# A recurrent branch pipelined one step ahead: the next input product in thirds between this step's gate products

## The reference, cut to what matters

```
z = xn @ w_in;  u_x, u_g, ... = split(z)
conv_in  = concatenate([conv_hist, u_x])              # 3 frames of history
u        = conv1d(conv_in, conv_w, width 4, per channel) + conv_b
r        = sigmoid(blockdiag(u, w_a) + b_a)           # 64 x 64 blocks
i        = sigmoid(blockdiag(u, w_x) + b_x)
log_a    = -8 * r * softplus(-lru_lambda);  a = exp(log_a)
b        = sqrt(-expm1(2 * log_a)) * (i * u)
h[t]     = a[t] * h[t-1] + b[t]                       # a scan along time
y        = gelu(u_g) * h                              # then @ w_rnn_out, elsewhere
```

## Time and profile before

| | us |
|---|---|
| median of 3 runs | 2535.72 |
| profiled execution, its own time | 2537.56 |
| its span, first to last instruction | 2535.7 |
| attention stages before the recurrent stage, up to about | 1268 |
| recurrent stage, first matmul 1269.27 to the next stage's first DMA 1535.98 | 266.7 |
| TensorE clock granted, mean over the span | 0.936 |

### The profile page before, as it was taken

How to read it: one execution, slowest core, us unless ns; L and a number is a source line. 1 busy time by engine, 2 the same in 40 slices (tenths; PEclk the granted TensorE clock), 3 DMA queues, 4 the chain that set the end, 5 groups by cost and what they waited for, 6 DMA issues and landing times. The chain is left out here.

```text
span 2535.7 us, 36826 instructions
## 1 busy us (share of the span) xinstructions
PE 2175.3 (86%) x11116; PEld 1764.4 (70%) x11116; DVE 1345.9 (53%) x1576; ACT 1130.0 (45%) x1539; POOL 227.3 (9%) x299
## 2 busy tenths in 40 slices
PE   4469898988889797699999998998938999999993
PEld 2357676766767674499988888997836777777772
DVE  5423635455463545421145563224266888888885
ACT  3223444435343443221146663113215777777771
POOL 0210202012020201000000000000000010100003
PEclk9779999999999997799999998999968999999996
DMA  3310302021120201121132323131138999999996
GB/s 92 68 36 10 86 9 77 25 61 42 44 76 9 69 25 36 57 89 42 33 89 89 91 85 122 41 131 67 42 118 288 393 394 395 392 398 392 398 392 243
DMA packets 199024, 351.66 MB, mean 139 GB/s; under 512 B 19700, under 2 KB 127400, under 8 KB 198872
## 3 DMA queue, kind: packets, MB, share of 16 engines
q1 hardware_dynamic: 181496, 293.55, 32.4%
q0 software_dynamic: 13872, 44.74, 5.8%
q10 hardware_dynamic: 3584, 12.58, 1.2%
HBM read 301.87 MB, written 48.97 MB: 138 GB/s over the span
## 5 line engine op out<-in xcount | busy, mean ns | idle before, releaser
L2466 DVE TENSOR_TENSOR e_w_lo<-e_raw,e_w_hi 128x2048 fp32r<-128x2048 f32 x189 | 427.6, 2290 | 83.2 <-ACT e_w_hi L2396 43.5
L2396 ACT CAST e_w_hi<-e_raw 128x2048 fp32r<-128x2048 f32 x189 | 360.9, 1911 | 50.6 <-PE e_y_ps L103 33.6
L101 PE MATMUL proj_ps<-w_qkv_hi,xh 128*128 128x384 f32 x544 | 233.1, 429 | 24.8 <-PEq L287 19.1
L101 PE MATMUL ux_ps<-xh,r_wx_hi 128*128 128x364 f32 x576 | 192.2, 334 | 25.6 <-DVE r_wx_lo L777 14.8
L102 PE MATMUL ux_ps<-xl,r_wx_hi 128*128 128x364 f32 x576 | 191.2, 332 | 0.0
L103 PE MATMUL ux_ps<-xh,r_wx_lo 128*128 128x364 f32 x576 | 191.1, 332 | 0.0
L103 PE MATMUL proj_ps<-w_qkv_hi,xl 128*128 128x384 f32 x544 | 188.4, 346 | 0.0
L102 PE MATMUL proj_ps<-w_qkv_lo,xh 128*128 128x384 f32 x544 | 188.2, 346 | 0.0
L1353 PE MATMUL out_ps<-mT 128*128 128x512 f32 (+3 forms) x384 | 170.9, 528 | 2.9 <-DVEq L84 2.3
L101 PEld LDWEIGHTS proj_ps<-w_qkv_hi,xh 128*128 128x128 f32 x544 | 106.9, 197 | 51.4 <-issue 45.2
L1552 ACT ACTIVATE mT<-st_ps 128x512 f32<-128x512 f32 x192 | 93.9, 489 | 103.8 <-PE st_ps L1338 48.8
(11 more groups left out here) (431 smaller groups left out, 5087.1 us busy)
## 6 DMA issues: line engine op xcount, KB each, us to landing
e_raw<-w_gate_e SPq DMA_DIRECT2D x64, 1024.0 KB, 7.3
e_raw<-w_up_e SPq DMA_DIRECT2D x64, 1024.0 KB, 7.9
e_raw<-w_down_e SPq DMA_DIRECT2D x64, 1024.0 KB, 7.4
w_raw<-w_in SPq DMA_DIRECT2D x24, 512.0 KB, 4.6
r_wx<-w_in SPq DMA_DIRECT2D x24, 512.0 KB, 3.9
slot_y<-e_y ACTq DMA_DIRECT2D x32, 384.0 KB, 6.1
slot_y<-zrows POOLq DMA_DIRECT2D x24, 368.0 KB, 4.4
mT<-cache_k SPq DMA_DIRECT2D x8, 1024.0 KB, 5.7
```

What stands on the lines that cost most here:

```text
L101: nc.tensor.matmul(out, a_hi, b_hi, start=start, stop=False)
L2396: sc.copy(w_hi[u][:, :], w.raw[c][:, :]).then_inc(wh_ready, 1)
L2466: v.tensor_tensor(w_lo[u][:, :], w.raw[c][:, :], w_hi[u][:, :], ALU.subtract).then_inc(wl_ready, 1)
```

## The change

PE runs the input product one step ahead and cuts it into three thirds. Behind each third it issues two of this step's six gate units. So its loop is now: gelu product of step c (`branch`), then third 0 of the input product of step c+1, gate units 0 and 1 of step c, third 1, units 2 and 3, third 2 (signals `ux_ready`), units 4 and 5. The input product of step 0 stands ahead of the loop; step 7 has only its gelu product and its six units.

ACT waits for the gelu product first, rounds the next g weights, loads the sigmoid table, does sigmoids 0 and 1, then gelu (moved from behind tanh), the sigmoid table again, sigmoids 2 and 3, the copies of the next step's `ux_ps` (`take_input`, for step c+1), sigmoids 4 and 5, exp, tanh, the rounding of the x weights of step c+2, and the square root. The wait for `step_done` moves from unit 0 to gelu and unit 3.

DVE does `rest_g` for c+1, i times u, then the convolution of step c+1 (`convolve`), then the two operations for the root, `rest_x` for step c+2, then i times the root, the scans and y. The chains are split: `chain_i` for the copies, `chain_u` for the convolution. SP and POOL keep their lists. The arithmetic of every operation is the same. The core of the diff (bodies that are only moved into functions are left out):

```diff
-        V_STEPS, A_STEPS = 19, 15
+        chain_u, chain_i = sem("r_chain_u"), sem("r_chain_i")
+        V_STEPS, U_STEPS, A_STEPS = 9, 10, 10
...
             @block.tensor
             def _(pe):
...
+                def gate_unit(c, m):
+                    if m == 0:
+                        pe.wait_ge(bd_loaded, c * 64 + 64)
+                        pe.wait_ge(u_ready, c + 1)
+                    c0, n = CHUNKS[m % 3]
+                    pe.wait_ge(gate_taken, c * GATE_UNITS + max(m - 1, 0) + 1)
+                    nc.tensor.matmul(gate_ps[:, m % 2, 0:n], bd[:, m // 3, :], u_sb[:, c0:c0 + n],
+                                     start=True, stop=True).then_inc(gate_ready, 1)
+
+                def branch(c):
+                    pe.wait_ge(g_split, c + 1)
+                    pe.wait_ge(gel_ready, c + 1)
                     for j in range(N_THIRDS):
+                        last = third_of(ug_ps, wg_split, j)
+                    last.then_inc(ug_ready, 1)
+
+                def next_input(c):
+                    pe.wait_ge(x_split, c + 2)
+                    pe.wait_ge(conv_ready, c + 2)
+                    for j in range(N_THIRDS):
+                        last = third_of(ux_ps, wx_split, j)
+                        if j == N_THIRDS - 1:
+                            last.then_inc(ux_ready, 1)
+                        for m in range(j * 2, j * 2 + 2):
+                            gate_unit(c, m)
...
+                with pe.Fori(0, KT - 1) as c:
+                    branch(c)
+                    next_input(c)
+                branch(KT - 1)
+                for m in range(GATE_UNITS):
+                    gate_unit(KT - 1, m)
...
+                def step(c, more, after):
+                    chain = Chain(act, chain_a, c * A_STEPS)
+                    vec = lambda v: g.chan[:, bass.ds(c + v * KT, 1)]
+                    act.wait_ge(ug_ready, c + 1)
                     if more:
+                        round_g(c + 1)
                     chain(nc.scalar.activation(warm[:, :], g.ident[:, 0:1], ACT.Sigmoid))
...
+                    unit(0)
+                    unit(1)
+                    if more:
+                        gelu()
+                    chain(nc.scalar.activation(warm[:, :], g.ident[:, 0:1], ACT.Sigmoid))
+                    unit(2)
+                    unit(3)
+                    if more:
+                        take_input(c + 1)
+                    unit(4)
+                    unit(5)
                     act.sem_inc(ri_ready, 1)
...
+                    if not more:
+                        gelu()
+                    if after is not None:
+                        after()
                     act.wait_ge(var_ready, c + 1)
                     chain(nc.scalar.activation(v_sb[:, :], v_sb[:, :], ACT.Sqrt, scale=-1.0), std_ready)
...
+                take_input(0)
+                round_x(1)
+                with act.Fori(0, KT - 2) as c:
+                    step(c, True, lambda: round_x(c + 2))
+                step(KT - 2, True, round_gate)
+                step(KT - 1, False, None)
...
+                def step(c, more, after):
+                    chain = Chain(dve, chain_v, c * V_STEPS)
+                    vec = lambda k: g.chan[:, bass.ds(c + k * KT, 1)]
                     if more:
+                        rest_g(c + 1)
                     dve.wait_ge(ri_ready, c + 1)
                     chain(v.tensor_tensor(i_sb[:, :], i_sb[:, :], u_sb[:, :], ALU.mult))
+                    if more:
+                        convolve(c + 1)
 
                     dve.wait_ge(at_ready, c * 2 + 2)
                     chain(v.tensor_tensor(v_sb[:, :], a_sb[:, :], a_sb[:, :], ALU.mult))
                     chain(v.scalar_tensor_tensor(v_sb[:, :], v_sb[:, :], 1.0, th_sb[:, :], ALU.add, ALU.mult), var_ready)
+                    if after is not None:
+                        after()
                     dve.wait_ge(std_ready, c + 1)
...
                 rest_g(0)
+                convolve(0)
+                rest_x(1)
+                with dve.Fori(0, KT - 2) as c:
+                    step(c, True, lambda: rest_x(c + 2))
+                step(KT - 2, True, rest_gate)
+                step(KT - 1, False, None)
```

## The result

| | before | after |
|---|---|---|
| median of 4 runs each, us | 2536.73 | 2559.36 |
| lowest to highest | 2534.19 to 2538.62 | 2558.36 to 2560.05 |
| span of the profiled execution | 2535.7 | 2556.7 |
| stage: first matmul to the next stage's first DMA | 266.7 (1269.27 to 1535.98) | 289.5 (1268.92 to 1558.43) |
| one step, us | 30.8 | 31.9 (the first), then 33.6 to 34.4 |

The ratio is 1.0092, 95% interval 1.0079 to 1.0105: slower by 0.9%. The medians differ by 22.6 us, and the stage alone became 22.8 us longer, which is all of it.

What follows compares the result with a forecast made beforehand. PE bounded the kernel before (busy 29.2 of 31.0 us per step); after, a 32.2 us loop through PE, ACT and DVE would. 2537.56 + 13.4 for the later stage end + 9.2 for the clock gave 2560 us, range 2547 to 2568.

Steps and rivals of the forecast that it cites:

- the rest of the path: Stage up to the end of y(7), without a clock change: 13.4 us later than before, giving 2551.0 us.
- part 6: PE's clock falls after each idle before third 0: 1.5 us in each of six loops, 9.2 us in all.
- Part 1: PE's order: waits for `gate_taken` vanish; third 0 to third 2 takes 15.4 us, a step 28.7 if PE never waits.
- Part 2: Loop between `next_input` calls through PE, ACT's copies and sigmoids, and DVE to `rest_x`: 32.2 us against 30.8.
- The idle: PE waits for `x_split` in front of each `next_input` but the first, about 3.4 us.
- Part 3: Nothing else is later: x load hidden by 5 us; gelu's wait for y costs nothing, 0.9 us in hand.
- Part 4: ACT's extra table load per step lies in idle time before the copies; costs nothing, without that cover 2.4 us.
- Part 5: Stage ends: y(6) at 1524.9 releases step 7's i sigmoids; y(7) ends at 1541.8, 13.4 us later than before.
- the fourth rival: Clock stays low 4.9 us or more per idle before third 0: 2564 us, 2568 with gate units stretched; chance 0.06.
- the one in which the clock stays up: Same loop, but the clock stays up or falls in few loops: 2551 us; chance 0.30.
- PE sets the pace: At the `x_split` wait before third 0: ACT and DVE's list fits under 13.4 us, loop 28.7, 2530 us; chance 0.06.

Runs made afterwards that it cites:

- the remainder moved: The changed kernel with DVE making the remainder of the x weights straight behind the convolution, ahead of the root's two operations; 2535.19 us, ratio 0.9994.
- early x weights: The changed kernel with x weights of step c+2 loaded before the gate-unit wait, rounded behind sigmoid 5, remainder made behind i times u; 2533.61 us, ratio 0.9993.
- early g weights: The kernel with early x weights, and ACT rounds the g weights of step c+2 ahead of the square root of step c; 2531.23 us, ratio 0.9977.
- the last two kernels: Early x and g weights plus an own tile for the last step's i sigmoids, 2531.91 us; early x and g plus one-column gelu behind sigmoid 1, 2522.42 us.
- The tile of its own: The kernel with early x and g weights, with the last step's i sigmoids going to a separate tile; 2531.91 us, ratio 0.9980.
- the last kernel: The kernel with early x and g weights plus a one-column gelu behind sigmoid 1 that loads gelu's table before y; 2522.42 us, ratio 0.9946.

## Why the prediction was right

2560 us were forecast and 2559.36 came; the mechanism is the one of the forecast in each part that a run could reach. That the number came within 1 us is luck: the price of the clock, put at 9.2 us, was 13.3, and the rest of the path, put at 13.4, was 9.1 (part 6).

- **Part 1, PE's own work.** Forecast 28.7 us a step, measured 31.93 - 3.99 = 27.94. The gate units were taken too long: units 4 and 5 with the switch take 0.99 us (1341.93 to 1342.92), where the sum had 1.5 at the most careful reading of the earlier trace rows. From the earlier trace rows a pair of 512 was put at 1.8 us and a 64 at 0.6; a 64 with a 512 unit takes about 1 us rather than 1.4.
- **Part 2, the loop.** Forecast 32.2 us, measured 31.93 in the one loop at full clock. PE's part with its handover was 14.98 us (15.4 + 0.14 forecast), ACT's 4.06 us (3.86 + 0.14 forecast) and DVE's with the handover to PE 12.89 (12.56 + 0.14). That `rest_x` at its new place sets it is shown by moving it: the loss is gone.
- **The idle** was 4.0 us for 3.4: PE's own work was 0.8 us shorter than forecast, the loop only 0.3 us.
- **Part 3.** ACT did wait for the x load, by 0.35 us in step 1, but over 6 us before DVE took the result. Gelu did not wait for y (its load starts 0.18 us behind sigmoid 1). It did in step 6 alone, 1.7 us, in the kernels with the remainder moved and with early x weights, and in six steps with early g weights.
- **Part 4, the tables.** Nothing, as forecast (289.5 us with and without two loads). The drain of which the Trainium skill speaks (page ScalarE: Activation LUTs, section What ACT_TABLE_LOAD costs) does not show here either: the operation that follows a load starts 0.01 to 0.02 us behind it in the rows above (gelu at 1360.21, its load from 1358.91 to 1360.19). But a load that stands behind a wait on a loop costs its full 1.28 us, which the last two kernels show (29.8 to 28.5).
- **Part 5, the end.** From y(6) to y(7): 16.8 us measured, 16.9 forecast; the first i sigmoid of step 7 was released by y, as forecast. y(6) came 38.5 us after `next_input(6)`, 36.2 without the clock's 2.3; the sum had 38.2, since it took the loop's durations for steps that are written out and have shorter gaps, and PE's work again.
- **Part 6, the clock.** It fell in all six, and cost more than the 1.5 us assumed: the six loops take 1495.56 - 1292.94 = 202.6 us for 6 x 31.93 = 191.6, 11.0 more, and step 6 another 2.3; 13.3 for 9.2 (6 x 1.5 is 9.0 in fact). The term was mis-sized because 3.4 us at the low level were taken from one row; here the clock returned after about 5 in five of the six. That is what the fourth rival (the clock stays low longer, chance 0.06) had: 6 x 2.2 = 13.2 us. Its time, 2564 us, did not come because the path was shorter. The rest of the path came to 9.1 us (22.4 of y(7)'s delay less 13.3) where 13.4 were forecast. The two errors, +4.1 and -4.3, cancel.

Of the rivals, the one in which the clock stays up lost by 8 us (2551), and it comes near the kernel with the idle filled (2552.39, of which 3.3 are the filler's own in step 0). "PE sets the pace" lost in this kernel, but its condition could be built: with the list behind third 2 taken apart the step is 28.5 us, half a microsecond from PE's own work, and the time 2522 us.

What stays open: whether the last step could be shortened too. The tile of its own moved one wait and met another, and no further kernel was made for it. Nor do the runs show where the last kernel gains the 5 us that its stage does not have, or why the clock fell after one of the waits of about 1.1 us and not after the others.

## What to carry to other kernels

When a step is pipelined one ahead, list for each product what the operation that feeds it now stands behind; a small operation (1.2 us of weight remainder) placed at the end of another engine's list put 17.1 us in series with the product, where 13.2 were covered. Loops hide one behind the other: after each repair add up the next (31.9, 30.1, 29.8, 28.5 here) before expecting the engine's own work as the step. And put anything that needs no data, such as a table load, ahead of the wait and not behind it.

## What the runs showed of the hardware that was not expected

In the kernel after, the granted clock fell in all six idle stretches of PE of 4.0 us or just behind them: in five before the idle was over, in one 1.3 us after it. Each fall cost 1.65 to 2.5 us of the following work, about half the length of the idle itself, on top of it. In the filler kernel 20 matmuls with no use, 3.5 us of them, left 0.65 us of idle; the clock stayed up in all six, and the stage was 9 us shorter. A short idle is not always safe, though. Six stretches of 1.1 to 1.5 us (the remainder moved) left the clock alone, but in each of the two kernels with early g weights at 29.8 us a step, one of five stretches of 0.8 to 1.2 us was followed by a fall. In the rows above it came 1.9 us after work had resumed and lasted 3.3 us.

A table load stands behind the wait of the activation that needs it: gelu's load started only when y was done (1358.91), after 2.40 us of idle. A one-column gelu ahead of the wait took it off the loop, 29.8 to 28.5 us per step.
